# 24 of 640 gather slots moved from the front of a fused decoder layer to its dense expert stage

## The reference, cut to what matters

```python
q = (yb @ w_q).reshape(PEER_CHUNK, PEER_HEADS, 2, PEER_HALF)
s = jnp.einsum('chpk,hpnk->chpn', q, sub_keys).astype(jnp.float32)
s1, i1 = lax.top_k(s[:, :, 0], PEER_TOPK)
s2, i2 = lax.top_k(s[:, :, 1], PEER_TOPK)
cand = (s1[..., :, None] + s2[..., None, :]).reshape(PEER_CHUNK, PEER_HEADS, PEER_TOPK * PEER_TOPK)
sc, ci = lax.top_k(cand, PEER_TOPK)
...
idx = row * PEER_KEYS + col
gate = jax.nn.softmax(sc, axis=-1)
act = jax.nn.gelu(jnp.einsum('ched,cd->che', u[idx], yb), approximate=False)
return jnp.einsum('che,ched->cd', (gate * act).astype(yb.dtype), v[idx])
```

## Time and profile before

| | us |
|---|---|
| median of three runs | 3172.87 |
| lowest and highest run | 3158.06, 3176.31 |
| the profiled execution, its own time | 3159.18 |
| its span, first to last instruction | 3157.3 |
| TensorE busy | 2871.0 |
| VectorE busy | 2479.8 |
| ScalarE busy | 962.6 |
| Pool busy | 925.6 |

### The profile page before, as it was taken

How to read it: one execution, slowest core, us unless ns; L and a number is a source line. 1 busy time by engine, 2 the same in 40 slices (tenths; PEclk the granted TensorE clock), 3 DMA queues, 4 the chain that set the end, 5 groups by cost and what they waited for, 6 DMA issues and landing times.

```text
span 3157.3 us, 31533 instructions
## 1 busy us (share of the span) xinstructions
PE 2871.0 (91%) x9793; PEld 1686.7 (53%) x9793; DVE 2479.8 (79%) x5164; ACT 962.6 (30%) x2681; POOL 925.6 (29%) x866
## 2 busy tenths in 40 slices
PE   9999999988887888888988887898999999999997
PEld 7785665544554445544555655343455545555553
DVE  2114778889899999889879997678877877877777
ACT  2311466611225555511145643111112111111110
POOL 1101244433333444433000012223323323333331
PEclk9999999999998999998999988999999999999999
DMA  5724989899999999899546478999999999999994
GB/s 181 261 104 179 343 328 347 329 404 365 419 405 381 330 337 329 318 406 356 190 147 231 177 275 326 391 390 389 414 392 404 402 398 401 393 410 414 404 403 196
DMA packets 225446, 1047.41 MB, mean 332 GB/s; under 512 B 23424, under 2 KB 70016, under 8 KB 141440
## 3 DMA queue, kind: packets, MB, share of 16 engines
q0 software_dynamic: 92160, 671.13, 54.1%
q1 hardware_dynamic: 132112, 374.13, 31.9%
q10 hardware_dynamic: 1008, 0.14, 0.0%
HBM read 995.50 MB, written 49.81 MB: 331 GB/s over the span
## 4 chain that ended last, share of the span: by engine, by line
PE 61%; DVE 21%; DMA 11%; issue 4%; ACT 2%; SPq 1%; POOL 0%; DVEq 0%; POOLq 0%; ACTq 0%
PE w_ps L1902 15%; PE r_o L1916 12%; PE w_ps L1670 11%; PE w_ps L1916 6%; DVE z_e L1557 5%; DVE ring L1599 4%; DMA ring<-uv,idx 3%; PE r_o L1848 3%; PE r_o L1670 3%; DMA gel_kept<-e_scr 2%; DMA ub<-uT 2%; DMA wc<-w_branch 2%; PE w_ps L1787 2%; DVE hot_r L1479 2%; PE w_ps L1848 1%
## 5 line engine op out<-in xcount | busy, mean ns | idle before, releaser
L920 POOL DMA_INDIRECT ring<-uv,idx x640 | 768.0, 1200 | 1913.7 <-DVE z_e L1557 1849.8
L1557 DVE SCALAR_TENSOR_TENSOR z_e<-ring,coef,z_e 128x1024 f32<-128x1024 f32 x640 | 819.6, 1281 | 193.9 <-ACT coef L1154 193.5
L1599 DVE CUSTOM_DVE_ANT_0 ring<-ring,ytok 128x1024 f32<-128x1024 f32 x640 | 778.3, 1216 | 22.6 <-DMA ring<-uv,idx 22.0
L1902 PE MATMUL w_ps<-yT,ub 128*128 128x384 f32 x2048 | 690.2, 492 | 11.4 <-DMA ub<-uT 11.4
L1902 PEld LDWEIGHTS w_ps<-yT,ub 128*128 128x128 f32 x2048 | 392.6, 193 | 300.5 <-issue 49.8
L1670 PE MATMUL w_ps<-x,w 128*128 128x384 f32 (+1 forms) x1632 | 488.6, 447 | 10.5 <-DMA x<-xT 6.5
L1670 PEld LDWEIGHTS w_ps<-x,w 128*128 128x128 f32 x1632 | 304.3, 193 | 150.1 <-issue 30.1
L1916 PE MATMUL r_o<-vb,gel_d 128*128 128x512 f32 x704 | 318.2, 595 | 5.5 <-DMA vb<-v 5.5
L1131 ACT ACTIVATE gel_d<-w_ps 128x384 f32<-128x384 f32 x92 | 45.2, 491 | 769.0 <-PE w_ps L1902 769.0
L1150 ACT ACTIVATE gel<-dot 128x2 f32<-128x2 f32 x320 | 64.0, 200 | 653.9 <-DVE dot L1599 653.2
L1916 PEld LDWEIGHTS r_o<-vb,gel_d 128*128 128x128 f32 x704 | 134.3, 191 | 156.6 <-issue 127.2
(11 more groups left out here) (251 smaller groups left out, 3310.2 us busy)
## 6 DMA issues: line engine op xcount, KB each, us to landing
w<-w_in SPq DMA_DIRECT2D x132, 512.0 KB
ub<-uT SPq DMA_DIRECT2D x128, 512.0 KB
vb<-v SPq DMA_DIRECT2D x128, 512.0 KB
g_scr<-stage_g SPq DMA_DIRECT2D x12, 2048.0 KB, 7.4
gq<-g_scr SPq DMA_DIRECT2D x16, 1536.0 KB
wq<-wq SPq DMA_DIRECT2D x46, 512.0 KB
wc<-w_branch SPq DMA_DIRECT2D x24, 768.0 KB, 6.1
wo<-w_out SPq DMA_DIRECT2D x24, 512.0 KB, 8.7
```

The lines of the kernel that those rows point to most:

```text
L920: nc.gpsimd.indirect_dma_start(out=ring[t % RING][:], out_offset=None, in_=a["uv"], in_offset=bass.IndirectOffsetOnAxis(ap=idx[:, slot:slo ...
L1557: nc.vector.scalar_tensor_tensor(z[n % 2][:], ring[t % RING][:, D:], coef[:, slot:slot + 1], z[n % 2][:], ALU.mult, ALU.add).then_inc(vsum ...
L1599: nc.vector.tensor_tensor_reduce(ring[r][:, 0:D], ring[r][:, 0:D], y_of(n)[:], 1.0, 0.0, ALU.mult, ALU.add, dot[:, slot:slot + 1]).then_in ...
L1902: ins = nc.tensor.matmul(dense_bank(b)[:, 0:DENSE], ub[b % NUB][:, c], yT[2][c // 4][:, c % 4, :], start=c == 0, stop=c == DC - 1)
```

## The change

Only the slots of the knots change; the ticks stay.

```diff
-KNOTS = ((0, 0), (96, T_N[1]), (109, SCORE_TIMES[1][0]), (137, UNIT_T[2][0]), (159, T_A[2]), (263, T_B[2]), (280, T_N[2]),
-         (293, SCORE_TIMES[2][0]), (300, FOUND_AT[0]), (318, FOUND_AT[-1]), (LAST_SLOT, T_END - 20))
+KNOTS = ((0, 0), (88, T_N[1]), (100, SCORE_TIMES[1][0]), (126, UNIT_T[2][0]), (146, T_A[2]), (242, T_B[2]), (258, T_N[2]),
+         (270, SCORE_TIMES[2][0]), (276, FOUND_AT[0]), (294, FOUND_AT[-1]), (LAST_SLOT, T_END - 20))
```

## The result

| kernel | median, us | ratio to the kernel before (95% interval) |
|---|---|---|
| before | 3169.65 | |
| changed | 3205.18 | 1.0137 (1.0115 to 1.0159) |

The change costs time, 1.4% by the ratio on record. That ratio is not the quotient of the two medians, which is 1.0112: the four runs of the kernel before spread from 3158 to 3176 us. Against its medians in the later rounds, 3158 to 3163 us with 17 or 19 runs each, 3205.18 is 1.013 to 1.015. The profiled execution of the changed kernel has a span of 3211.0 us, 53.7 more than that of before. Here is its table by stretch, cut at its own knots (products 71, 88, 100, 126, 146, 242, 258, 276, 294, 320 and 374), the columns as in the earlier trace rows; the last two rows run from product 294 to the start of the parted sums, and over these.

What follows compares the result with a forecast made beforehand. Bounds were taken by stretch: TensorE, DMA or VectorE in front, TensorE with DMA just behind in the dense stage. Front -44 and dense stage +33 gave -11 us, so 3155 us; range 3120 to 3190, the forecast's own 3135 to 3172.

Steps and rivals of the forecast that it cites:

- 1 slot, first norm: 723 to 777 us, VectorE busy 51.47 of 54: one slot fewer gains 2.5 us, within 0 to 3.
- 8 slots, attention: 946 to 1347 us, attention of the last group, bound by VectorE: eight slots fewer gain 16 us, within 12 to 24.
- 1 slot, branches: 1347 to 1415 us, bound by DMA at 418 GB/s: one slot fewer gains 2 us, within 1 to 3.
- 2 slots, to the search: 1415 to 1494 us, VectorE 72.98 of 79: two slots fewer gain 4 us, within 0 to 6.
- front: 305 to 1494 us: fewer slots gain 44 us in sum, low ends 22, high ends 66.
- 1831 to the first gate: Start of the dense stage, 1831 to 2006 us: more slots lose 4 us on VectorE and 2 on DMA.
- parted blocks: 2006 to 2205 us, blocks whose scores were parked, DMA share 1.00: 3.7 slots more lose 8 us, 10 at most.
- later blocks: Dense stage, 2205 to 3123 us: 18.5 slots more make DMA the bound and lose 19 us.
- the term of 2205 to 3123: Dense stage: 425 GB/s asked of a DMA taken to sustain 416, so 918 us grow by 2.1%, 19 us.
- Rival 1: Dense stage, 2205 to 3123: DMA sustains only 404 GB/s; losses 63 against 44 gained, +19, 3178 us; chance 0.20.
- Rival 2: Dense stage: DMA has room and carries 425 GB/s; losses 10 against 44 gained, -34, 3125 us; chance 0.22.
- Rival 3: Front gives only its low ends, 22 us, as the chain moves to TensorE and ScalarE; +11, 3170; chance 0.18.

Runs made afterwards that it cites:

- e10: Changed kernel with each gq load in four parts 1.5 blocks apart and a fourth ub buffer: 3157.89 us, ratio 0.9984 to the kernel before.
- e13: Changed kernel with the whole gq loads issued through ScalarE's queue instead of SP's: 3161.86 us, ratio 1.0000 to the kernel before.

## Why the prediction was wrong

By its own steps, as gains and losses in us (measured between the products and gates that bound each stretch, in one execution of each kernel; a row of 2 us or less is within the rounding):

| step | predicted | measured |
|---|---|---|
| to product 77 (71) | 5 | 5 |
| to product 96 (88) | 4 | 5 |
| 1 slot, first norm | 2.5 | -5 |
| 2 slots, scores | 5 | 7 |
| 2 slots, first units | 5.5 | 3 |
| 8 slots, attention | 16 | 17 |
| 1 slot, branches | 2 | -2 |
| 2 slots, to the search | 4 | 2 |
| front | 44 | 33 |
| 1831 to the first gate | -6 | -5 |
| parted blocks | -8 | -6 |
| later blocks | -19 | -72 |
| the end | 0 | -2 |

**Right**: the front as a whole, 33 us within 22 to 66 though 11 below the 44 of the sum, and its largest term (8 slots of attention brought 17 us for 16; VectorE was the bound there). Of the stretches that were to gain a little, those with a norm or the branches in them lost 5 and 2 us. There the chain passes loads in turn with steps of the engines, and fewer slots may bring nothing; no run tested this. The parted blocks and the search tail came near what was worked out.

**Wrong**: the term of 2205 to 3123. The prediction put the DMA's sustained rate at 416 GB/s and took the time as demand over rate. Two things were off. The first is a size: the mixed stream with gq carries 410 to 411, not 416 (e10, e13), and the demand over these blocks is 427 to 432, not 425. By its own formula 410 and 427 give 38 us instead of 19. With the stalls out of the way the changed kernel's later blocks lose 942 - 905 = 37 us against the kernel before without its own stalls. Against the kernel before as it was they lose 942 - 925 = 17 us; that this is almost the 19 predicted is luck, since 20 us of stalls in the kernel before, which the prediction did not count, make up for the rate. The second is a step that was missing: the loads of gq were not looked at as items of SP's queue. The sentence "these queues have slack in every stretch ... I cost them at nothing" was the one that failed. The rows that it names have no column for SP at all, and the share of a queue's busy time would not be the delay of one urgent issue in it either. What the runs showed in its place: a gq load in SP's queue holds the next issue for up to 19 us, its 1 KB packets take that queue's turns, and the load of ub behind it comes up to 17 us late for TensorE, after 7 of 11 gq loads. That costs 997 - 942 = 55 us, which e13 gave back.

**Rival 1** had the right place and sign, and its evidence, the 21.55 us load, was the right row. But its mechanism was a low sustained rate, 404; what was there is a rate that is high (413 GB/s in the stall) or nearly nothing (137 GB/s behind it), so that the mean fell to 392, below the rate of before, and the loss was larger than its 47. (The 406 GB/s below which it was to decide is the rate of a clear loss of 16 us; by the same sums front and dense stage break even at 412, above what e10 and e13 carry.) Rival 2 was wrong as long as gq is loaded: no run carries 425, and without gq 412 is all that is asked for. Rival 3 was wrong on the front, which gave 33, half way between the forecast's 44 and its 22.

The measured 3205 lies 15 us above the range, whose upper end rested on 404 as the worst rate. A closed loop that stands still can go below any rate seen in a stretch without stalls.

## What to carry to other kernels

Before more traffic is put on a DMA that is nearly full, read the timeline of the issuing queue, also where its engine has no busy time in the tables: an issue that takes many times its usual length says that the next load is late however early it was meant to be. Then count packets and bytes by queue over the same stretch. Cut or move the large load made of small pieces that stands in front of urgent ones, to another queue or into parts spaced by the work that consumes them; that was worth more here than the question of how many slots lie where. And where engines wait for each other in a ring (a load, TensorE, a gelu, coefficients, buffers, gathers), cost a late load not by the wait it ends but by all that stands still with it.

## What the runs showed of the hardware

- Behind a load of 1536 KB in 1 KB packets the issue of the next one in the same queue took 6 to 19 us while the DMA was full (10 of 11 times in the changed kernel; 8 to 16 us, 5 of 11 times, in the kernel before), and none took over 0.5 us when the large load came from another engine's queue (e13).
- The queues took turns by packet, not by bytes: over 20 us at 411 GB/s two queues moved 992 packets each, one 7.21 MB mostly in 8 KB packets and the other 1.02 MB in 1 KB packets, and three queues moved 694, 681 and 692 (e13).
- The carried rate over more than 900 us at full load is 410 to 411 GB/s with the gq loads in the stream; stretches without them reach 418 and 419 in the earlier trace rows.
- TensorE's granted clock fell to 0.56 while it stood for 15 us and was 0.92 over the 15 us after; the scoring block behind the gap took 8.3 instead of 5.3 us.
